# First slot's products side by side, second chunk's norm ahead of Silu, seven idle products, later k groups, six squares added

## What is computed

```python
x = x + 0.5 * swiglu(rmsnorm(x, ffn1_norm), ffn1_w1, ffn1_w3, ffn1_w2)   # d_ff 2816
x = x + hybrid_mixer(rmsnorm(x, mix_norm), w_in, ...)                    # q, k, v, r, a, u, gates
x = x + cross_attention(rmsnorm(x, xa_norm), rmsnorm(mem, mem_norm), wq, wk, wv, wo)
x = x + 0.5 * swiglu(rmsnorm(x, ffn2_norm), ffn2_w1, ffn2_w3, ffn2_w2)
return rmsnorm(x, final_norm)
# rmsnorm(x, g) = x * rsqrt(mean(x * x) + 1e-6) * g;  swiglu(h) = (silu(h @ w1) * (h @ w3)) @ w2
```

## Time and profile before

| | value |
|---|---|
| median of 3 runs | 3143.51 us (3142.95 to 3742.75) |
| the profiled execution, whole | 3143.91 us |
| its span, slowest core (core 2) | 3142.0 us |
| spans of the odd cores / of the even cores | 3133.7 to 3134.4 / 3140.6 to 3142.0 us |
| PE busy in core 2 | 3081.2 us, 98% |
| DVE / ACT / POOL busy | 1185.6 / 950.6 / 480.5 us |
| mean granted clock of PE, core 2 | 0.996 |

### The profile page before, as it was taken

The page is one execution under the profiler, slowest core; times in us unless marked ns, Lnnn a source line. Parts: engine busy times, 40 slices in busy tenths (PEclk is TensorE's granted clock), DMA queues, the critical chain, the costliest instruction groups (busy, mean ns, idle before and its releaser), DMA issues.

```text
span 3142.0 us, 42848 instructions; the slowest of 8 cores (3133.7 to 3142.0 us)
## 1 busy us (share of the span) xinstructions
PE 3081.2 (98%) x15047; PEld 1448.3 (46%) x15350; DVE 1185.6 (38%) x1880; ACT 950.6 (30%) x1637; POOL 480.5 (15%) x557
## 2 busy tenths in 40 slices
PE   6999999999999999999999999999999999999998
PEld 2544544444444454444444445444444444544443
DVE  2223744522321473541332156363232226536212
ACT  3122532521211253342121136153212114425211
POOL 0012111121201120122110112022120021112002
PEclk9999999999999999999999999999999999999999
DMA  8797343344753634334384455233457344322434
GB/s 169 119 160 126 63 91 118 60 74 79 141 98 65 105 69 84 108 68 86 58 173 73 73 92 108 49 113 62 88 102 145 64 84 89 81 68 55 89 69 105
DMA packets 56784, 292.32 MB, mean 93 GB/s; under 512 B 5632, under 2 KB 11136, under 8 KB 32256
## 3 DMA queue, kind: packets, MB, share of 16 engines
q0 software_dynamic: 39024, 251.35, 44.4%
q1 hardware_dynamic: 17552, 38.21, 3.8%
HBM read 495.78 MB, written 22.02 MB: 165 GB/s over the span
## 4 chain that ended last, share of the span: by engine, by line
PE 95%; DMA 2%; issue 1%; DVE 1%; ACT 1%; DVEq 0%; SPq 0%; ACTq 0%; POOLq 0%
PE psum_all L107 95%; DMA sb_slot<-w_in 1%; DMA sb_slot<-ffn_w 1%; PE psum_all L123 1%; DMA ov_xin<-x 0%; DVE sb_hT L419 0%; DVE sb_xT L419 0%; ACT ov_rawb L388 0%; DVE ov_kT L790 0%; DVE ov_kT L702 0%; ACT ov_zb L775 0%; DVE ov_nmx L1021 0%; ACT ov_rstd L413 0%; ACT ov_rstd L411 0%; ACT ov_uT L692 0%
## 5 line engine op out<-in xcount | busy, mean ns | idle before, releaser
L107 PE MATMUL psum_all<-sb_hT,sb_slot 128*128 128x512 bf16 x7507 | 1678.9, 380 | 29.8 <-DMA sb_slot<-ffn_w 7.7
L107 PEld LDWEIGHTS psum_all<-sb_hT,sb_slot 128*128 128x128 bf16 x7680 | 750.3, 98 | 922.0 <-issue 35.1
L107 PE MATMUL psum_all<-ov_gated,sb_slot 128*128 128x512 bf16 x2760 | 608.7, 379 | 3.6 <-DMA sb_slot<-ffn_w 0.6
L520 DVE TENSOR_TENSOR ov_gated<-psum_all,ov_sl 128x512 bf16<-128x512 f32 x352 | 243.3, 691 | 922.1 <-PE psum_all L107 869.2
L517 ACT ACTIVATE ov_sl<-psum_all 128x512 bf16<-128x512 f32 x352 | 210.2, 597 | 906.1 <-PE psum_all L107 857.7
L107 PEld LDWEIGHTS psum_all<-ov_gated,sb_slot 128*128 128x128 bf16 x2816 | 275.5, 98 | 333.3 <-issue 1.6
L388 ACT ACTIVATE ov_sqt<-sb_xT 128x512 bf16<-128x512 f32 x224 | 140.4, 629 | 545.5 <-DVE sb_xT L541 215.4
L395 POOL TENSOR_TENSOR ov_acc<-ov_acc,ov_sqt 128x512 f32<-128x512 f32 x180 | 212.1, 1178 | 480.1 <-ACT ov_sqt L388 477.4
L135 POOL DMA_DIRECT2D sb_slot<-ffn_w x176 | 95.5, 544 | 1222.0 <-PE psum_all L107 1076.5
L107 PE MATMUL psum_all<-sb_slot,sb_hT 128*128 128x512 bf16 x1002 | 232.1, 379 | 1.6 <-ACT ov_uT L692 0.5
L419 DVE SCALAR_TENSOR_TENSOR sb_hT<-sb_xT,sb_small,ov_rstd 128x512 bf16<-128x512 f32 x192 | 140.8, 792 | 30.2 <-ACT ov_rstd L413 30.2
(11 more groups left out here) (138 smaller groups left out, 1999.5 us busy)
## 6 DMA issues: line engine op xcount, KB each, us to landing
sb_slot<-ffn_w POOLq DMA_DIRECT2D x88, 1024.0 KB, 11.7
sb_slot<-ffn_w POOLq DMA_DIRECT2D x88, 704.0 KB, 7.3
sb_slot<-w_in POOLq DMA_DIRECT2D x40, 1024.0 KB, 13.1
out<-sb_xT SPq DMA_DIRECT2D x14, 1024.0 KB, 16.7
ov_xin<-x SPq DMA_DIRECT2D x12, 1024.0 KB, 13.7
sb_slot<-w_up_a POOLq DMA_DIRECT2D x8, 1024.0 KB, 13.1
sb_slot<-w_mix_out POOLq DMA_DIRECT2D x8, 1024.0 KB, 11.1
sb_slot<-kq_s POOLq DMA_DIRECT2D x8, 1024.0 KB, 5.1
```

Of the source, the lines that this page charges most:

```text
L107: ("ins", (lambda e, o=o, l=l, r=r, st=st, sp=sp: e.matmul(o, l, r, start=st, stop=sp)), i == n - 1)
L520: S.op("dve", lambda e, b3=b3, slt=slt, j=j, s=s: e.tensor_tensor(out=gated[:, j, sl(s)], in0=b3[:], in1=slt[:], op=ALU.mult), [bb3, slb[0 ...
```

## The change

Five edits.

1. The first slot of the first `ffn` goes through a function of its own, `first_pair`. The four groups of a chunk (w1 and w3 for jj = 0, 1) fill four banks side by side: for each `kc` four products, one to each bank, then the next `kc`. Silu and multiply follow the four groups.
2. The squares of the second chunk (`n1.sq_all`) stand right behind the first chunk's norm, and its `ones`, `stat` and `apply` behind the four groups of the first chunk and ahead of all Silu. `raw1` moves from 36 KB to 90 KB in the arena. `steady(7, raw1)` adds seven products between `ones` and the second chunk's products; they go to bank 7, and nothing reads them.
3. `k_group(m, 0)` stands one q group later, so that two q groups come first and two k groups last.
4. `k_group(m, 1)` is taken out of PSUM by ACT instead of DVE.
5. `nx1` of the mixer's output and of `oproj` have `chain=6` instead of 4.

```diff
+    def steady(n, raws):
+        bk, bb = psum_at(7)
+        for i in range(n):
+            t_, tb = raws[i % 8]
+            S.mm([(bk[:], onesD[:], t_[:], True, True)], tb + CB, [bb])
+
+    def first_pair(st, sbuf, gate):
+        sv = v3(st, 8, 512)
+        def products(s, bks):
+            for kc in range(8):
+                S.mm([(bk[:], sv[:, kc, c * 128:(c + 1) * 128], hT[:, kc, sl(s)], kc == 0, kc == 7)
+                      for c, (bk, _) in enumerate(bks)], [sbuf, hT_b[s][kc]], [bb for _, bb in bks])
+        def gates(s, bks):
+            for jj in range(2):
+                gate(jj, s, *bks[jj], *bks[2 + jj])
+        b0 = [psum() for _ in range(4)]
+        products(0, b0)
...
+        n1.ones()
+        n1.stat()
+        steady(7, raw1)
+        n1.apply()
...
+        gates(0, b0)
+        b1 = [psum() for _ in range(3)] + [(n1.bk, n1.bb)]
+        products(1, b1)
+        gates(1, b1)
...
+            if first and pi == 0:
+                first_pair(*got[0], gate)
+                continue
...
         def k_group(m, s):
             bk, bb = group(wk_, m, s)
-            S.op("dve", lambda e: e.tensor_copy(out=kTt[:, m, sl(s)], in_=bk[:]), [bb], kT_b[s * 4:s * 4 + 4])
+            if s == 0:
+                S.op("dve", lambda e: e.tensor_copy(out=kTt[:, m, sl(s)], in_=bk[:]), [bb], kT_b[s * 4:s * 4 + 4])
+            else:
+                S.op("act", lambda e: e.activation(out=kTt[:, m, sl(s)], in_=bk[:], func=AF.Copy),
+                     [bb], kT_b[s * 4:s * 4 + 4])
...
+        q_group(0, 0)
         for m in range(4):
-            q_group(m, 0)
+            if m < 3:
+                q_group(m + 1, 0)
             k_group(m, 0)
             pool(m, 0)
...
-        nx1 = xnorm(O_G_XA, 1, bank=4, chain=4)
+        nx1 = xnorm(O_G_XA, 1, bank=4, chain=6)
...
-        nx1 = xnorm(O_G_FFN2, 1, chain=4)
+        nx1 = xnorm(O_G_FFN2, 1, chain=6)
...
     n1 = first_norm(1, chain=0, raws=raw1)
-    deferred += [n1.sq_all, n1.rest]
+    n1.sq_all()
```

More of the change, by code:

```diff
@@ L263, in build_program @@
     raw0 = [ov(f"rawa{i}", 46 + i, [128, SUB], BF16) for i in range(8)]
-    raw1 = [ov(f"rawb{i}", 36 + i, [128, SUB], BF16) for i in range(8)]
+    raw1 = [ov(f"rawb{i}", 90 + i, [128, SUB], BF16) for i in range(8)]
     rawm = [ov(f"rawm{i}", 90 + i * 0.5, [128, MEM], BF16) for i in range(8)]
@@ L491, in hgroup, with gate @@
             S.mm([(bk[:], lhs_fn(kc), hT[:, kc, sl(s)], kc == 0, kc == 7)], [sbuf, hT_b[s][kc]], [bb])
+    def gate(j, s, b1, bb1, b3, bb3):
+        slt, slb = sl_t[(j * NSUB + s) % 2]
+        S.op("act", lambda e: e.activation(out=slt[:], in_=b1[:], func=AF.Silu), [bb1], [slb[0]])
+        S.op("dve", lambda e: e.tensor_tensor(out=gated[:, j, sl(s)], in0=b3[:], in1=slt[:], op=ALU.mult),
+             [bb3, slb[0]], [gated_b[j * NSUB + s]])
+    def steady(n, raws):
[14 more added lines that the diff above has]
+        products(0, b0)
+        lab = S.label
+        S.label = "ffn0/dnorm"
+        n1.ones()
+        n1.stat()
+        steady(7, raw1)
+        n1.apply()
+        S.label = lab
+        gates(0, b0)
+        b1 = [psum() for _ in range(3)] + [(n1.bk, n1.bb)]
+        products(1, b1)
+        gates(1, b1)
     def ffn(l, x_in, hooks, nxt, between=(), drip=()):
@@ L515, in ffn @@
                                sbuf, s, False)
-                        slt, slb = sl_t[(j * NSUB + s) % 2]
-                        S.op("act", lambda e, b1=b1, slt=slt: e.activation(out=slt[:], in_=b1[:], func=AF.Silu),
-                             [bb1], [slb[0]])
-                        gb = gated_b[j * NSUB + s]
-                        S.op("dve", lambda e, b3=b3, slt=slt, j=j, s=s: e.tensor_tensor(
-                            out=gated[:, j, sl(s)], in0=b3[:], in1=slt[:], op=ALU.mult),
-                            [bb3, slb[0]], [gb])
-                        if s == 0 and j == 0 and first:
-                            deferred.pop(0)()
+                        gate(j, s, b1, bb1, b3, bb3)
                         if s == 0 and j == (1 if first else 0):
```

## The result

The changed kernel took **3127.31 us** (median of six runs, 3125.93 to 3127.98); its ratio to the kernel before is 0.9948, 95% interval 0.9936 to 0.9960. That is 16.2 us or half a per cent less. The forecast was 3123.5 us, 20 less. Both the interval and the two ranges of times, which lie 14 us apart, say that it is faster. The kernel before was executed again beside each experiment: over 30 executions (3139.6 to 3143.95) its median is 3142.1, and measured from that the gain is 14.8 us. Some executions, of any of the kernels, ran with the clock of two or more cores held down for long stretches; they are left out of every time given here, and where one was profiled, PE is read on its other cores.

A forecast was written before the change was run, and what follows sets the result against it. PE, busy 3081.2 of 3142.0 us on core 2, was taken as the bound. Gains of 7.3 + 3.5 + 1.7 + 4.3 + 3.4 = 20.2 us off 3143.5 gave 3123.3, rounded up to 3123.5; range 3119 to 3131.5.

The forecast's parts named there:

- The bound, and core 2: Whole kernel: PE, busy 3081.2 of 3142.0 us, bounds it; core 2 sets the time and gains 20.2 us.
- the k weights: Mixer, core 2: one more q group ahead of the first k group hides late k weight loads, 3.5 us.
- the clock at the second mixer: After the 2.08 us wait on core 2: with a shorter gap PE's clock stays up, giving back 1.7 us.
- k by ACT: Each tile's mixer: ACT empties k's bank, removing PE's wait of 1.08 us, four times, 4.3 us.
- the sums: Two norms in each of four tiles: three `ones` products instead of five, 16 products fewer, 3.4 us.
- the 0.36: Late k weights, core 2: what stays of the 2.08 us wait after 1.72 us are hidden.
- The slowest stays near 3122: All cores at the end: core 2 at 3121.8, odd cores at 3119.4, other even cores like core 2.
- The start: First slot, second chunk: an earlier norm and side-by-side groups start its last product at 42.45 instead of 49.72, 7.3 us.
- Nothing replaces the wait: Mixer, after k's evacuation: the next needed bank is free by 341.3, PE comes at 342.1; the 4.3 us gain stands.
- Clock falls anyway: Rival, first slot: clock falls in the remaining gap before the second chunk, 4.4 us more, 3127.9; chance 0.15.
- Lead lost to loads: Rival, after the first slot: late loads take back the start's 7.3 us, 3130.8; chance 0.07.
- k weights still late: Rival, mixer: k weight loads follow their own pace, 5.2 us less gain, 3128.7; chance 0.08.

The follow-up runs named there:

- ring_plus_one: The changed kernel with one PSUM bank drawn and left unused after the first slot; ratio 0.9951, in a second series 3124.93 us (ratio 0.9947).

## Why the prediction missed, point by point

- **The bound, and core 2: right.** 19.7 us against 20.2. The terms for the k weights, the clock at the second mixer, k by ACT and the sums hold: 12.9 us from the first `ov_aT` to the end of core 2, as the four terms have it, though the new wait of 0.95 is in it. The 1.24 of k by ACT against 1.08, and the 0.36, make up for it. The 2.08 us wait vanished whole where 0.36 were to stay.
- **"The slowest stays near 3122": this is the step that failed.** I took one execution's two groups of cores, took their terms off ("Odd cores: 3134.4 − 15.0 = 3119.4"), and let the slowest of the result set the time. The odd cores got 9.6 us in the mean, not 15.0, and the slowest of them, core 1, got 8.5. Beside the 0.95 of the new wait, four things took part, odd cores in the mean: the first product 1.35 us later (23.50 against 22.15; cores 1, 3 and 7), 1.14 less of the start's term, 0.65 more of late feed-forward loads, 0.85 more in the last stores. With 0.95 that makes 4.9 of the missing 5.4. Over all eight cores of the two profiles the gain was 14.0 where the terms make 17.6 (20.2 and 15.0, half each), and most of the missing 3.7 struck every core: 0.95 of the new wait, 0.9 of the start, 0.9 in the last stores, against 0.7 for the later first product. The rest of the miss is the maximum over chance. The two groups themselves were a draw of one execution: late k weights struck one core of a pair, sometimes the even one and sometimes the odd one, and stood above everything else. Once they were gone, the slowest of eight was whichever core drew the worst lateness, in the mean 2.3 us above the mean of the eight. For that the sum had no term.
- **The start: a little too large.** Forecast 7.3, measured 6.84 on core 2 (36.09 for PE's return where 35.8 was forecast: Ln began 0.2 later than I had it, and PE 0.1 later behind `apply`) and 6.4 in the mean over the cores, counted from each core's first product. The gap before was 3.76 us on all eight cores, but the slot time differed with the clock's loss, 11.4 to 13.1 us; on core 2, from which I read it, it was 12.7.
- **"Nothing replaces the wait": right for k, wrong for the banks.** The order of the banks was looked at for k's bank and for the first slot. That the first slot draws one bank fewer than before, and so shifts all that follow in the tile, was not counted. `ring_plus_one` shows that it was this: 0.95 us.
- **The end.** The last `ov_aT` to the end gained 1.9 on core 2 as forecast, and nothing on core 1. The stretch behind the last product was taken as constant, because eight cores showed it so; it was constant only because the cores of a pair came there apart.
- **The rivals.** Clock falls anyway: no; and its price was too high (up to 1.7, not 4.4). Lead lost to loads: no, 0.75 us in both. k weights still late: no. Banks in turn: no. Another wait in place of one removed: in part, 0.95 us, from a place that was not named. Second chunk of x late: no, its last square ends at 29.1 to 31.4 us on the eight cores. What came late, on three cores, was the last piece of the first chunk, at a cost of 1 to 3 us; no rival had it.
- **Two per cent as what can be told from no change: wrong.** The six executions of the changed kernel lie within 2.1 us, 30 of the kernel before within 4.4, and the ratio came with an interval of a quarter of a per cent. A forecast 0.6% below before meant "faster", and the chances should have said so.

## What to carry to other kernels

When products wait on an operand that arrives piece by piece, lay several groups side by side over free banks, four here: this was worth about 5 us at the end of one slot, and 3.4 us of the kernel's time, for no additional work. When the metric is the slowest of several cores and some of them are slower for a single reason, removing that reason uncovers a maximum over chance; put a term for it into the sum, read from how far equal cores scatter over several executions. One profile can show a pattern, such as even cores against odd ones, that the next execution does not have. And when an edit changes how many buffers of a ring are drawn, walk the ring to its next fixed bank, since a shift by one can bring back a wait far away.

## What the hardware showed unexpectedly

- The last stores of two neighbouring cores (0 and 1, 2 and 3, ...) slow each other: about 250 GB/s for stretches instead of 380 alone, up to 2.2 us at the end of a span (10.9 us against 8.7). Cores brought to the same pace meet there.
- The granted clock fell to 0.50 (1.2 GHz) after PE had resumed from a gap of 2.70 us, on six cores of eight, with the same program and the same gap; after 1.19 us it stayed at 1.00 on all eight where products followed without a break, and fell where they followed one by one at DVE's pace.
- A load issued 2 us earlier can go with a late landing of one issued before it: x's last square ended up to 7 us later on six of 12 cores on which the first slot's load was issued before 8 us, and on none of the other 92.
- A weight load that came late on one core of a pair came in time, or at most 0.4 us late, on its neighbour: of 16 pairs in four profiles, 15 had one core that lost more than 0.8 us by it, none had two, and which core it was changed with the execution.
